# Attention of one query chunk woven with the projections of the next and with the gating unit, exp(scores) as weights of the value product

## The reference, cut to what matters

```python
h = rmsnorm(x, norm1_g)
q, k, v, f_logit, u, sv, gates = split(h @ w_in)        # 512, 512, 512, 8, 512, 512, 2048 columns
logf = log_sigmoid(f_logit + b_f)                       # cumulated along the sequence: c
logits = q_t . k_s / 8 + c_t - c_s                      # 8 heads x 64, causal
y_a = (softmax(logits) @ v) @ w_a
y_b = (gelu(u) * (W_s layernorm(gelu(sv)) + b_s)) @ w_b # windows of 128, 8 groups x 64
x = x + (sigmoid(g_a) * y_a + sigmoid(g_b) * y_b) @ w_o
x = x + square(relu(rmsnorm(x, norm2_g) @ w_up)) @ w_down
out = rmsnorm(x, normf_g)                               # x is (4, 4096, 1024), float32
```

## Time and profile before

| | before |
|---|---|
| median of 3 runs | 1262.06 us |
| profiled execution, its own time | 1260.61 us |
| span of its slowest core (core 4) | 1259.1 us |
| the other cores' spans | 1256.0 to 1258.8 us |
| TensorE, VectorE, ScalarE, GpSimd busy | 94%, 44%, 43%, 18% |
| projections, 0 to 197 us | 197.0 us, TensorE busy 167.34 |
| gating unit and forget sums, to 286.3 us | 89.3 us, TensorE busy 73.81 |
| attention, to 562 us | 275.7 us, ScalarE busy 257.85, TensorE 264.66 |
| merge, `w_o`, MLP, last norm, to 1259.1 us | 697.1 us, TensorE busy 678.90 |

### The profile page before, as it was taken

How to read it: one execution, slowest core, us unless ns; L and a number is a source line. 1 busy time by engine, 2 the same in 40 slices (tenths; PEclk the granted TensorE clock), 3 DMA queues, 4 the chain that set the end, 5 groups by cost and what they waited for, 6 DMA issues and landing times.

```text
span 1259.1 us, 18676 instructions; the slowest of 8 cores (1256.0 to 1259.1 us)
## 1 busy us (share of the span) xinstructions
...
## 2 busy tenths in 40 slices
...
GB/s 211 191 72 130 68 68 7 48 1 93 45 46 45 41 42 30 32 19 111 69 45 37 15 161 116 67 1 67 39 29 68 1 67 1 67 34 34 2 70 199
DMA packets 22847, 78.40 MB, mean 62 GB/s; under 512 B 4032, under 2 KB 4896, under 8 KB 17168
## 3 DMA queue, kind: packets, MB, share of 16 engines
...
q10 hardware_dynamic: 288, 0.03, 0.0%
...
## 4 chain that ended last, share of the span: by engine, by line
PE 88%; DMA 3%; DVE 3%; ACT 2%; issue 2%; POOL 1%; DVEq 0%; ACTq 0%; POOLq 0%; SPq 0%
PE pss L359 88%; DMA WQ<-wproj 3%; ACT sq L363 1%; ACT PT L363 1%; DVE st L620 1%; DVE x1T L371 1%; ACT L363 0%; POOL vln L371 0%; DVE ostg L377 0%; DVE rec L780 0%; DMA rec<-scr 0%; DVE stmp L371 0%; DMA out<-ostg 0%; DMA scr<-ysb 0%; DVE xfin L374 0%
## 5 line engine op out<-in xcount | busy, mean ns | idle before, releaser
L371 DVE TENSOR_TENSOR x1T<-pss,x1T 128x512 f32<-128x512 f32 x256 | 176.4, 691 | 247.5 <-PE pss L359 219.0
L363 ACT ACTIVATE PT<-pss 128x1024 bf16<-128x1024 f32 (+1 forms) x320 | 256.6, 943 | 16.2 <-PE pss L359 16.2
L359 PE MATMUL pss<-aT,fdn 128*128 128x512 bf16 x1024 | 226.7, 379 | 0.6 <-DVE x1T L371 0.6
L359 PE MATMUL pss<-h2T,fup 128*128 128x512 bf16 x1024 | 226.2, 379 | 0.0
L363 ACT ACTIVATE rl<-pss 128x512 f32<-128x512 f32 x128 | 76.3, 597 | 333.3 <-PE pss L359 327.6
L371 POOL TENSOR_TENSOR aT<-rl 128x512 bf16<-128x512 f32 x128 | 133.8, 1046 | 264.4 <-ACT rl L363 251.5
L359 PE MATMUL pss<-PT,VP 128*65 128x512 bf16 (+7 forms) x640 | 170.3, 347 | 10.8 <-ACT PT L363 9.4
L359 PE MATMUL pss<-QpT,KpT 86*128 86x512 bf16 (+3 forms) x640 | 170.6, 350 | 0.3 <-issue 0.2
L359 PEld LDWEIGHTS pss<-aT,fdn 128*128 128x128 bf16 x1024 | 100.1, 98 | 121.7 <-issue 1.6
L359 PEld LDWEIGHTS pss<-h2T,fup 128*128 128x128 bf16 x1024 | 100.2, 98 | 120.8
L780 DVE RECIPROCAL rec<-rec 64x512 f32<-64x512 f32 x32 | 107.1, 3348 | 57.1 <-DMA rec<-scr 56.9
...
## 6 DMA issues: line engine op xcount, KB each, us to landing
xbuf<-xown SPq DMA_DIRECT2D x8, 1024.0 KB, 6.5
xbuf<-xprev SPq DMA_DIRECT2D x8, 1024.0 KB, 5.1
...
fup<-w_up POOLq DMA_DIRECT2D x8, 1024.0 KB, 9.5
fdn<-w_down POOLq DMA_DIRECT2D x8, 1024.0 KB, 9.8
...
KpT<-KT SPq DMA_DIRECT2D x8, 512.0 KB, 5.0
```

What stands on the lines that cost most here:

```text
L359: S.op("pe", lambda e, a=(out, lhsT, rhs, start, stop): e.matmul(a[0], a[1], a[2], start=a[3], stop=a[4]), r, w)
L363: S.op("act", lambda e, a=(out, in_, func, scale): e.activation(out=a[0], in_=a[1], func=a[2], scale=a[3]), r, w)
L371: S.op(eng, lambda e, a=(out, in0, in1, op): e.tensor_tensor(a[0], a[1], a[2], a[3]), r, w)
```

## The change

Four things are done at once.

The value product is turned round. `PT`, 128 keys by 128 queries, is now the weights, and V with its ones column, 65 columns, is streamed. The output has the queries on partitions, four pieces of 65 columns in one bank. The denominator is then a column, so that `rec` is a reciprocal of 128x4, `yst` the product with it, and after each pair of heads `tr` turns `yst` back with 4 matmuls by the identity. The way over DRAM goes.

The loop order is chunk, then head. Scores of chunk I need only keys of chunks 0 to I, so attention of chunk I is emitted between pieces of the projections of chunk I+1, and in the last chunk between pieces of the gating unit. `fill` is the list of these pieces (half units of 4 matmuls), and a running account (`acc`) sets how many stand in each step. The four stretches are called windows 0 to 3 below. Scores have two pairs of banks in place of three, the pieces two banks (`ring`), the outputs two. The diagonal groups of a chunk are packed as 1024, 1024 and 512 columns in place of 1024, 768, 512 and 256.

K no longer stays in SBUF: each unit goes by `kst` to DRAM (`scrt`), and `headload` reads it back for each of the 32 pairs of chunk and head, at the chunk's length. The first loads are put in a row (x of position 0, WV, WK, x of position 1, WQ) by making each wait for the one ahead of it.

The gating unit's Gelu becomes a tanh form: a copy and two or three `stt` on VectorE, a square on GpSimd, Tanh on ScalarE. The layernorm's power stands on GpSimd and its scaling on VectorE. The casts of V and Q go from ScalarE to VectorE, and 10 of 16 squares of x to GpSimd. In the later stages only places in SBUF differ, and `xres` has 5 buffers in place of 7.

```diff
+        ld("pool", WV[:], wproj_d[0], B("WV"), [B("xb01")])
         ld("pool", WK[:], wproj_d[1], B("WK"))
-        xload(1)
-        ld("act", bfb[:], bf_d[0:1, :].broadcast_to([128, 32]), B("bfb"))
-        ld("pool", WQ[:], wproj_d[2], B("WQ"))
+        xload(1, [B("WK")])
+        ld("pool", WQ[:], wproj_d[2], B("WQ"), [B("xb11")])
...
+        def squares(pos, engs):
...
+            for hf, eng in enumerate(engs):
+                src, dst = xbuf[i_][:, hf * 2048:(hf + 1) * 2048], sq[:, hf * 2048:(hf + 1) * 2048]
+                if eng == "act":
+                    act(dst, src, AF.Square, [B("xb%d%d" % (i_, hf))], [B("sq%d" % hf)])
+                else:
+                    tt(eng, dst, src, src, ALU.mult, [B("xb%d%d" % (i_, hf))], [B("sq%d" % hf)])
...
+            def evict(pv):
+                pv4 = ps(pv).rearrange("p (q e d) -> p q e d", e=2, d=64)
+                cp("dve", VP4[:, gb, :, 0:64], pv4[:, :, 0, :], [PB[pv]], [B("VP%d" % gb)])
+                cp("dve", VP4[:, gb, :, 65:129], pv4[:, :, 1, :], [PB[pv]], [B("VP%d" % gb)])
...
+                    ki = ksn[0] % 4
+                    ksn[0] += 1
+                    cp("dve", kst[ki][:], ps(pb), [PB[pb]], [B("kst%d" % ki)])
+                    S.dma("sp", lambda e, a=(scrt_d[p, :, ci * 512:(ci + 1) * 512], kst[ki][:]): e.dma_start(out=a[0], in_=a[1]),
...
+        def headload(n):
+            I, h = divmod(n, NH)
+            kb, p, r0 = n % 2, h // 2, 64 * (h % 2)
+            w = 512 * (I + 1)
+            o2 = lambda ap: ap.rearrange("p (o t) -> p o t", o=2)[:, :, 0:w]
+            cs = [o * 4 + i for o in range(2) for i in range(I + 1)]
+            qs = slice(I * 512, (I + 1) * 512)
+            ld("sp", o2(KpT[kb][0:64, :]), o2(scrt_d[p, r0:r0 + 64, :]), B("Kd%d" % kb), [B("scrt%d_%d" % (p, ci)) for ci in cs])
+            ld("sp", QpT[kb][0:64, qs], QT[r0:r0 + 64, p * T + I * 512:p * T + (I + 1) * 512], B("Qd%d" % kb), [B("QT%d_%d" % (p, I))])
+            ld("sp", o2(KpT[kb][64:64 + NAUG, :]), o2(scrk_d[h * NAUG:(h + 1) * NAUG, :]), B("Ka%d" % kb), [B("scrk%d" % ci) for ci in cs])
+            ld("sp", QpT[kb][64:64 + NAUG, qs], scrq_d[h * NAUG:(h + 1) * NAUG, qs], B("Qa%d" % kb), [B("scrq%d" % I)])
...
+        def gelu_pre(pb, i3):
+            x_, xB, z_, zB = xs[i3], B("xs%d" % i3), zz[i3], B("zz%d" % i3)
+            cp("dve", x_[:], ps(pb), [PB[pb]], [xB])
+            tt("pool", z_[:], x_[:], x_[:], ALU.mult, [xB], [zB])
+            return x_, xB, z_, zB
+
+        def gelu_mid(z_, zB, x_, xB):
+            stt(z_[:], z_[:], 1.0 / TC, x_[:], ALU.add, ALU.mult, [zB, xB], [zB])
+            act(z_[:], z_[:], AF.Tanh, [zB], [zB], scale=TK * TC)
...
+                x_, xB, z_, zB = gelu_pre(pb, i3)
+                late.append([2, lambda: gelu_mid(z_, zB, x_, xB)])
+
+                def fin():
+                    gt, gB = gg[b % 2], B("gg%d" % (b % 2))
+                    s6, s6B, b4 = st6[b % 2], B("st6%d" % (b % 2)), b % 4
+                    stt(gt[:], z_[:], 1.0, x_[:], ALU.add, ALU.mult, [zB, xB], [gB])
+                    S.op("dve", lambda e, a=(s6[:, 0:6], gt[:]): e.bn_stats(a[0], a[1]), [gB], [s6B])
+                    S.op("dve", lambda e, a=(mv[b4][:, 0:2], s6[:, 0:6]): e.bn_aggr(a[0], a[1]), [s6B], [B("mv%d" % b4)])
+                    ts("dve", tv[b4][:], mv[b4][:, 1:2], 4.0 * EPS, None, ALU.add, ALU.bypass, [B("mv%d" % b4)], [B("tv%d" % b4)])
+                    tt("pool", rsv[b4][:], tv[b4][:], mhalf[:], ALU.pow, [B("tv%d" % b4), B("mhalf")], [B("rsv%d" % b4)])
+
+                def nrm():
+                    gt, gB, b4 = gg[b % 2], B("gg%d" % (b % 2)), b % 4
+                    ts("dve", gt[:], gt[:], mv[b4][:, 0:1], rsv[b4][:, 0:1], ALU.subtract, ALU.mult, [gB, B("mv%d" % b4), B("rsv%d" % b4)], [gB])
+                    tt("pool", vln[b % 6][:], gt[:], lng[:], ALU.mult, [gB, B("lng")], [B("vln%d" % (b % 6))])
+                    vdone.add(b)
...
+        def chunk_list(c):
+            o, e = 2 * c, 2 * c + 1
+            qs = []
+            if c == 1:
+                qs += rms_q(o)
+                qs += ev(lambda: squares(e, ("act", "pool")))
+                qs += stt_q(o) + ev(lambda: xload(o + 2))
+                qs += f_q(o) + kq_q(o, 0, False)
+                qs += rms_q(e)
+                qs += ev(lambda: squares(o + 2, ("pool", "pool")))
+                qs += weave(kq_q(o, 0, True) + kq_q(o, 1, False), stt_q(e), 2)
+                qs += ev(lambda: xload(e + 2))
+                k1 = False
+            else:
+                qs += kq_q(o, 0, False)
+                k1 = True
...
+            t2 = kq_q(o, 2, False) + kq_q(e, 2, False) + kq_q(o, 2, True)
+            if c < 3:
+                qs += rms_q(o + 2) + ev(lambda: squares(e + 2, ("pool", "pool")))
+                qs += weave(t2, stt_q(o + 2), 2)
...
+                qs += f_q(o + 2)
+                qs += kq_q(o, 3, False) + kq_q(e, 3, False)
+                qs += rms_q(e + 2)
+                if c < 2:
+                    qs += ev(lambda: squares(o + 4, ("pool", "pool")))
+                qs += weave(kq_q(o, 3, True) + [("pair", (c, 3))] + kq_q(o + 2, 0, True), stt_q(e + 2), 2)
...
+        def sgu_list():
+            qs = ev(bias2)
+            for b in range(16):
+                qs += u_q(b) + sv_q(b)
+                if b >= 5:
+                    qs += mix_q(b - 5)
...
+        def wload():
+            ld("pool", WU[:], wproj_d[3], B("WU"))
...
+            ot, ow = 4 * I, 16 + 4 * I
+            gl.append([(ot, 0, 0, 0, False), (ow, 0, 1, 0, True)])
+            gl.append([(ot + 1, 128, 0, 0, False), (ot + 3, 384, 0, 384, False), (ow + 1, 128, 1, 0, True), (ow + 3, 384, 1, 384, True)])
+            gl.append([(ot + 2, 256, 0, 0, False), (ow + 2, 256, 0, 256, True)])
+            for gi, g in enumerate(gl):
+                steps.append((n, g, gi, gi == len(gl) - 1, 2 if gi < len(gl) - 1 else 1))
...
+            n, g, gi, last, nb = steps[k]
+            I, h = divmod(n, NH)
+            yb = 4 + n % 2
+            first = gi == 0
+            tot = [(s_, qb) for s_ in g for qb in range(s_[1] // 128, 4)]
+            for i, ((j, q0, bi, co, dg), qb) in enumerate(tot):
+                o0 = bi * 512 + co + qb * 128 - q0
+                mm(pss[:, yb * 512 + qb * 65:yb * 512 + (qb + 1) * 65], PT[k % 3][:, o0:o0 + 128], slab(j, h),
+                   first and i == 0, last and i == len(tot) - 1, [B("VP%d" % j), B("VPo"), B("PT%d" % (k % 3))], [PB[yb]])
...
+                S.op("dve", lambda e_, a=(rec[ri][:, :], y3[:, :, dc_]): e_.reciprocal(a[0], a[1]), [PB[yb]], [B("rec%d" % ri)])
+                tt("dve", yst[yi][:, :].rearrange("p (q c) -> p q c", c=128)[:, :, 64 * e:64 * e + 64], y3[:, :, d0:d0 + 64],
+                   rec[ri][:, :].unsqueeze(2).broadcast_to([128, 4, 64]), ALU.mult, [PB[yb], B("rec%d" % ri)], [B("yst%d" % yi)])
+                if e:
+                    def tr():
+                        p = h // 2
+                        for qb in range(4):
+                            mm(pss[:, yb * 512 + qb * 128:yb * 512 + (qb + 1) * 128], yst[yi][:, qb * 128:(qb + 1) * 128], identb[:], True, True,
+                               [B("yst%d" % yi), B("identb")], [PB[yb]])
+                        cp("dve", yaT[:, p * T + I * 512:p * T + (I + 1) * 512], ps(yb), [PB[yb]], [B("ya%d_%d" % (p, I))])
+                    pend.append((k + 2, tr))
...
+            acc += cost_w[I] / wsum[I] / frac[I] * (0.94 if nb == 2 else 0.52)
+            while fill and acc > 0.0 and not (fill[0] == ("win", I + 1) and I < 3):
+                acc -= pop_fill()
```

More of the change, by code:

```diff
@@ new lines, in build @@
+        squares(1, ("act", "act"))
+        for p in range(4):
+            run(kq_q(0, p, False))
+        run(rms_q(1))
+        run(stt_q(1))
+        xload(3)
+        run(f_q(1))
+        run(kq_q(1, 0, False))
+        run(fin_tot(0))
+        run(kq_q(1, 1, False))
+        run(fin_cum(0))
+        run(kq_q(1, 2, False))
+        for kind in range(3):
+            run(fin_tr(0, kind))
+        run(kq_q(1, 3, False))
+        run(v_q(1, 0))
+        run(kq_q(0, 0, True))
+        headload(0)
@@ L803, in build @@
-        while pending:
-            pending.pop(0)[1]()
+            if k + 1 < G and steps[k + 1][0] // NH != I:
+                ensure(("win", I + 1))
+                acc = 0.0
+                if I == 2:
+                    wload()
+        while fill:
+            pop_fill()
+        while late:
+            late.popleft()[1]()
+        while pend:
+            pend.pop(0)[1]()
         k = 0
```

757 lines of the change are left out of this document (384 added, 373 removed).

## The result

The changed kernel takes 1331.38 us (median of four runs, 1324.32 to 1502.48; a fifth took 1328.58) against 1262.06 for before in the same comparison. The ratio is 1.0529, 95% interval [1.0479, 1.0578]. I had said 1179, and faster. The profiled execution took 1336.07 us with a span of 1334.5 on core 7; the spans of the cores lie between 1314.7 and 1334.5, where before they lay within some 3 us.

A forecast was written before the change was run, and what follows sets the result against it. TensorE was taken as the bound in every window: 414.8 us of work plus 64 lost make 478.8 before the merge instead of 562.0, with 697.1 after it unchanged. That gave 1179 us, range 1146 to 1216.

The forecast's parts named there:

- the price of the small matmul: Value product: 2176 matmuls of 65 columns at 29.0 ns each, 63.1 us in place of 117.8, weight loads staying hidden.
- C: Rival on the value product: 65 columns cost as much as 128, 57 us more, time 1236; chance 0.05.
- D: Rival on the value product: each small matmul pays its weight load, 98 ns, so 150 us more, time 1329; chance 0.03.
- E: Rival in window 3: Tanh and Exp keep changing ScalarE's table, up to 64 loads, 82 us, time 1236; chance 0.03.
- the question is how much it waits: All windows: TensorE needs more time than ScalarE and becomes the bound, so only its waits, 64 us before the merge, matter.
- The signs that I had named for being wrong: Window 0 losing over 30 us, windows 1 and 2 held by ScalarE or loads, or the merge's 697.1 moving by over 3.
- Beginning: Ahead of attention: 27 us lost, between 20 and 39, in place of 38.7, as loads in a row let V and K start sooner.
- Window 0: Window 0: 15 us idle, between 6 and 30; about 9 for the norms of positions 2 and 3, 6 for head loads.
- Windows 1 and 2: Windows 1 and 2: 4 us lost in each, between 1 and 12, with more time for head loads and slack on ScalarE.
- Window 3: Window 3: 14 us lost, 10%, between 3 and 35, with three in-order engines at 90% or more beside TensorE's 140.4 us.
- rival B: Window 3 held by VectorE and ScalarE together at 175 us, 12 more in windows 0 and 1, time 1212; chance 0.22.
- After the merge: From the merge on: no change, 697.1 us stays, and xres with 5 buffers costs nothing.

The follow-up runs named there:

- e7: The changed kernel with the norms of positions 2 and 3 beside K and Q units and their x loads after K's stores: 1330.74 us, ratio 1.0532.
- e12: Kernel of e2, e3, e5, e6, e7, seven xres buffers and four gating blocks in window 2, with position 1's x awaiting WV, WQ awaiting WK: 1244.86 us.
- e2: The changed kernel with VPo, the ones column's buffer, taken out of what a value product reads: 1310.69 us, ratio 1.0373.
- e5: The changed kernel with the loads of WU and WSV held back until window 2 has its second pair of heads: 1318.16 us, ratio 1.0439.
- e3: The changed kernel with the gating unit's Tanh, its use and the scaling each one piece of the weave later: 1295.99 us, ratio 1.0247.
- e6: The changed kernel with each head's K and Q loads asked for two steps earlier in the list: 1333.11 us, ratio 1.0549.

## Why the prediction was wrong

*Right: the price of the small matmul, and the work.* 29.0 ns assumed, 30 to 31 measured, twice; that is 2 to 4 us over the kernel. Rivals C and D are out by the starts of the matmuls. D's time, 1329, is nearly the measured one by accident: its mechanism has no part in it. The sustained 81 ns of the Trainium skill (TensorE: Matmul & The Clock Gate, "Back-to-back issue gap") are not what this trace shows for 128x128 weights and 65 columns, 31 ns.

*Right: no table changes.* The profile has four table loads in all, so E is out. That agrees with the Trainium skill (ScalarE: Activation LUTs, "Table sets: the hidden batching unit"), which has tanh and exp in one set.

*Wrong: "the question is how much it waits".* That step failed, in all its terms. It gave 64 us of loss before the merge; 212.4 came. The signs that I had named for being wrong came too: window 0 lost over 30, window 1 (not 2) was held by loads in part (14.8 of its 26.1 idle us), and the time from the merge on moved by over 3. The largest excesses over my terms are window 3's (56.5 us), window 1's (34.0) and window 0's (25.5). By its terms:

- Beginning, 27 (at most 39): 49.3, of which 35.5 idle: 13.3 for `onesb`, as before, 12.1 behind the `stt` of two norms, 8.8 for `xfin` and 1.4 for a square. V began at 24.80 us, not at 17 to 20 and later than before's 22.67. `WV` had landed at 23.37; V stands behind the `wf` matmuls, and these wait for the norm's eight `stt`, the last at 24.13. (17 us was never to be had: before's first `stt` begins at 18.85.) V and K of position 0 then ran without a gap, as forecast. But the row order that I counted as a gain made the loads a chain, each link waiting for the one ahead, and the x of position 1 was asked for only at 30.24:

```profile
24.80 9.29 PE L362 MATMUL pss<-WV,hown 128*128 128x512 bf16 x32
...
30.24 0.80 SPq L390 DMA_DIRECT2D xbuf<-xprev  x2
...
33.92 7.07 PE L362 MATMUL pss<-hown,WK 128*128 128x512 bf16 x32
...
41.17 1.91 ACT L366 ACTIVATE sq<-xbuf 128x2048 bf16<-128x2048 f32 x1 [1.54 <-DMA xbuf<-xprev]
...
41.62 0.53 POOL L390 DMA_DIRECT2D WQ<-wproj  x1 [27.25 <-DMA xbuf<-xprev]
...
45.86 5.39 DVE L380 SCALAR_TENSOR_TENSOR hprev<-xbuf,gains,rstd 128x512 bf16<-128x512 f32 x8 [4.06 <-ACT rstd L366]
...
52.06 3.57 PE L362 MATMUL pss<-hprev,WK 128*128 128x512 bf16 x8
...
52.88 0.92 SPq L390 DMA_DIRECT2D xbuf<-xown  x2
...
53.89 2.27 SPq L542 DMA_DIRECT2D scrt<-kst  x4
...
65.51 0.69 DVE L384 CAST kst<-pss 128x512 bf16<-128x512 f32 x1 [13.01 <-DMA scrt<-kst]
...
69.17 0.66 PE L362 MATMUL pss<-xfin,onesf 32*128 32x64 f32 x2 [8.79 <-DVE xfin L374]
```

  From the end of K at 41 us to 52.06 TensorE has little but the squares' product, while position 1's norm follows its late x. The x load of position 2 waits for `WQ` on SP's queue until 52.88, the stores of K behind it wait too and land only at 65.42, behind that x (64.84), so VectorE's fifth cast waits 13.01 us for a free buffer, and `xfin` behind that cast on VectorE costs TensorE 8.79. e7 undid this last part, and attention began 8.0 us sooner. Of the loads' own order e12 loosened two links, for 1.0 us; the `wf` matmuls ahead of V, and the link of `WV` to x, were not tried.
- Window 0, 15 (at most 30): 40.5. I priced 9 us for the norms' uncovered `stt` and 6 for the head loads. The waits for `stt` were 12.9 us and those for head loads 1.4; 8.9 more stood behind VectorE's copies of `VP`, `QT` and `kst`, which I had not priced. TensorE's small `wf` matmuls come one by one behind eight `stt` of 0.66 us, as the first of them here:

```profile
97.79 0.17 PE L362 MATMUL pss<-wf,hown 128*128 128x8 bf16 x1 [4.44 <-DVE hown L380]
98.45 0.17 PE L362 MATMUL pss<-wf,hown 128*128 128x8 bf16 x1 [0.50 <-DVE hown L380]
```

  What I had left out as well is the clock. Its mean was 0.85 over the window, in which such waits come again and again; the granted level is 1.2 or 2.4 GHz, and at the lower one 8 matmuls of 512 columns take 3.57 us in place of 1.89. In window 0 "over" is 15.9 us, and in window 2, with hardly a wait and a clock of 1.00, it is 5.9. No run changed the clock by itself, so what it costs is not separated from the short waits.
- Windows 1 and 2, 4 each (at most 12): 38.0 and 14.1. The false dependency on `VPo` (e2, 13.1 and 6.7) and the two weight loads beside the head's own (e5, 12.3).
- Window 3, 14 (at most 35): 70.5, the largest miss. My rival B had the chain that ruled, "every `stt` comes late, so does Tanh, and the exponentials behind it", and TensorE's 37.1 us of waits for `PT` are over the 20 that I had set for it. But I took the chain for a result of the engines' load, priced it at 175 us, and put "a VectorE busy 95%" beside it; VectorE was busy 134.41 of 210.9 us, 64%. With nearly the same work and Tanh one piece later the window takes 172.1 (e3): 38.8 us were the place in the queue. That B's 175 lies near these 172.1 is luck, since e3 has little of that chain left.
- After the merge, nothing: 10.2. "`xres` with 5 buffers ... nothing" was wrong; VectorE waits for a load of `xres` and TensorE behind it

```profile
815.98 1.90 DVE L374 TENSOR_TENSOR x1T<-pss,xres 128x512 f32<-128x512 f32 x3 [5.90 <-DMA xres<-xown]
...
817.54 0.59 PE L362 MATMUL pss<-sq,onesb 128*128 128x512 bf16 x1 [6.22 <-ACT sq L366]
```

  and seven buffers bring back some 7: TensorE waited 4.4 to 7.7 us for `sq` in each of the eight kernels with five, and at most 0.5 in those with seven.

The deeper fault was to take TensorE's work as the floor of each window and add waits to it, one for each that I could name. The weave has chains of four in-order engines and two DMA queues in each piece. Five things went wrong at once, each in its own place, and their gains add; my range ended at 1216 because I let only one go wrong at a time. Only e6 and e7 show a wait that hid another. And with all five mended the stretch still loses 134.7 us, twice my 64: what could be won of it, and how much of it is the clock, stays open.
